# Two-layer transformer stack with a chunked recurrence: small triangular inverses taken off TensorE, in an eight-pair loop

## What is computed

```python
def step(state, inp):                      # 16 heads of width 64
    r_t, w_t, k_t, v_t, aa_t, bb_t = inp   # aa = -kk, bb = kk * a
    sa = jnp.einsum('bhvk,bhk->bhv', state, aa_t)
    state = state * w_t[:, :, None, :] + sa[..., None] * bb_t[:, :, None, :] + v_t[..., None] * k_t[:, :, None, :]
    return state, jnp.einsum('bhvk,bhk->bhv', state, r_t)
y = scan(step, ...); y = group_norm(y) * lnx_w + lnx_b; out = (y + bonus) * g
```

## Time and profile before

| | us |
|---|---|
| median of the three runs (lowest, highest) | 2082.74 (2081.55, 2086.68) |
| profiled execution, its own time | 2081.08 |
| its span | 2079.3 |
| PE busy | 2031.4 (98%) |
| PEld busy | 1678.5 (81%) |
| DVE busy | 1139.5 (55%) |
| ACT busy | 536.0 (26%) |
| POOL busy | 1178.7 (57%) |

### The profile page before, as it was taken

How to read it: one execution, slowest core, us unless ns; L and a number is a source line. 1 busy time by engine, 2 the same in 40 slices (tenths; PEclk the granted TensorE clock), 3 DMA queues, 4 the chain that set the end, 5 groups by cost and what they waited for, 6 DMA issues and landing times.

```text
span 2079.3 us, 39898 instructions
## 1 busy us (share of the span) xinstructions
PE 2031.4 (98%) x16195; PEld 1678.5 (81%) x16195; DVE 1139.5 (55%) x1533; ACT 536.0 (26%) x1139; POOL 1178.7 (57%) x1175
## 2 busy tenths in 40 slices
PE   8999999999999999999999999999999999999998
PEld 6888888877877787788877888888886888888886
DVE  6878624466667654202068677666773655555312
ACT  2100002233434212313143133333223023333101
POOL 6888865634534475545547044433374867677764
PEclk9999999999999999999999999999999999999999
DMA  3323331353353422311323022111223432332231
GB/s 136 102 92 102 101 101 46 92 176 121 127 163 112 148 82 64 98 62 61 124 56 93 15 65 66 46 48 46 65 65 124 133 101 81 101 99 90 89 112 56
DMA packets 181243, 190.28 MB, mean 92 GB/s; under 512 B 8526, under 2 KB 162269, under 8 KB 180829
## 3 DMA queue, kind: packets, MB, share of 16 engines
q1 hardware_dynamic: 172288, 181.81, 27.6%
q10 hardware_dynamic: 8796, 6.21, 1.0%
HBM read 179.56 MB, written 8.44 MB: 90 GB/s over the span
## 4 chain that ended last, share of the span: by engine, by line
PE 61%; DVE 3%; issue 1%; POOL 1%; DVEq 1%; POOLq 1%; ACT 0%; ACTq 0%
PE bank L915 8%; PE bank L916 8%; PE bank L917 8%; PE bank L1592 7%; PE bank L1553 3%; PE bank L1405 3%; PE bank L1421 2%; PE bank L1423 2%; PE bank L1422 2%; PE bank L1690 2%; PE bank L1327 1%; PE bank L1328 1%; PE bank L1329 1%; PE bank L1080 1%; PE bank L1294 1%
## 5 line engine op out<-in xcount | busy, mean ns | idle before, releaser
L740 POOL TENSOR_SCALAR whi<-raws 128x1024 fp32r<-128x1024 f32 (+5 forms) x312 | 321.0, 1029 | 284.9 <-PE bank L1082 166.8
L746 POOL TENSOR_TENSOR wlo<-raws,whi 128x512 fp32r<-128x512 f32 (+5 forms) x312 | 400.8, 1285 | 0.0
L745 POOL TENSOR_TENSOR wlo<-raws,whi 128x512 fp32r<-128x512 f32 (+5 forms) x312 | 373.4, 1197 | 46.0 <-issue 3.0
L915 PE MATMUL bank<-hbuf,whi 128*128 128x512 f32 (+2 forms) x840 | 329.4, 392 | 1.8 <-POOL wlo L746 1.8
L917 PE MATMUL bank<-hbuf,wlo 128*128 128x512 f32 (+2 forms) x840 | 327.8, 390 | 0.0
L916 PE MATMUL bank<-hbuf,whi 128*128 128x512 f32 (+2 forms) x776 | 303.0, 390 | 0.0
L649 POOL TENSOR_TENSOR spare<-ones 1x1 f32<-1x1 f32 x92 | 21.4, 233 | 298.5 <-PE bank L917 208.2
L915 PEld LDWEIGHTS bank<-hbuf,whi 128*128 128x128 f32 (+2 forms) x840 | 157.1, 187 | 37.0 <-POOL wlo L746 3.1
L917 PEld LDWEIGHTS bank<-hbuf,wlo 128*128 128x128 f32 (+2 forms) x840 | 157.1, 187 | 34.1
L916 PEld LDWEIGHTS bank<-hbuf,whi 128*128 128x128 f32 (+2 forms) x776 | 145.2, 187 | 31.1
L672 POOL TENSOR_SCALAR lg2L<-lg 128x128 fp32r<-128x128 f32 x8 | 2.4, 298 | 221.7 <-DMA lg<-in_g 221.7
(11 more groups left out here) (544 smaller groups left out, 4747.1 us busy)
## 6 DMA issues: line engine op xcount, KB each, us to landing
adaw<-in_w_ada SPq DMA_DIRECT2D x64, 384.0 KB, 4.3
raws<-in_w_up SPq DMA_DIRECT2D x22, 1024.0 KB, 4.9
raws<-in_w_in SPq DMA_DIRECT2D x41, 512.0 KB, 3.9
raws<-in_w_in SPq DMA_DIRECT2D x18, 1024.0 KB, 5.0
raws<-in_pool_w_in SPq DMA_DIRECT2D x16, 1024.0 KB, 5.4
raws<-in_mla_w_in SPq DMA_DIRECT2D x10, 1024.0 KB, 6.2
raws<-in_pool_w_out SPq DMA_DIRECT2D x8, 1024.0 KB, 5.1
raws<-in_mla_w_out SPq DMA_DIRECT2D x8, 1024.0 KB, 5.4
```

Source lines behind the costliest of these rows:

```text
L740: G.tensor_scalar(h_, r_, 1.0, 1.0, ALU.mult, ALU.mult)
L745: G.tensor_tensor(first[0], first[1], f32(first[2]), ALU.subtract)
L746: G.tensor_tensor(last[0], last[1], f32(last[2]), ALU.subtract).then_inc(raw_split, 1)
L915: M.matmul(dst, wh, acts[k][0], start=(first and k == 0), stop=False)
```

## The change

1. The 16x16 diagonal blocks are no longer inverted by products. `LEVELS` has four levels with five products instead of nine with 13. The gram "D" is masked and packed by DVE (`diagonal_blocks`) into 128x128, written to DRAM by a DMA on ACT's queue in runs of 16 elements, and read back so that each of 64 partitions holds one 16x16 block (`blocks_gathered`); DVE inverts the 64 blocks elementwise (`inverted_blocks`), the result and its transpose go to DRAM (`blocks_kept`) and come back in runs of 16 elements, 2048 of them (`blocks_spread`), and DVE spreads them over the 64x64 layout (`spread_blocks`).
2. "D" is computed inside gates(q), after 6 of its 48 matmuls (`D_AFTER`), instead of in slot 1 of the chain. DVE signals `rk.ab` as soon as the two operands of D are there.
3. The other steps of `prepare` are placed anew: slots 1, 2, 6, 7, 9, 10, 12, 14, 16, 17, 19, 21 hold one product each, the others none (before: 1 to 17, 19, 20, 21, 23).
4. Tiles of the decay and key part that lay in SBUF now lie in PSUM: sums of decays and `grown` in bank 5, key lengths, directions and modified keys in bank 3, the deviation in bank 4. The decay's constant factor goes into the scales of ACT's exponentials (one DVE instruction less, one sigmoid on ACT more); `kk` is no longer stored.
5. DVE's group norm is cut in two: `deviations(p)` (reciprocal, first product) after the decayed keys, `finished(p)` inside the next preparation.
6. Waits and banks follow (gate banks (0, 7) for all later pairs; `key_norms` waits for `rk.bon`, the chain for `gn.x`).

The core of the diff, with the other edits cut:

```diff
-    (("DA", "D", "N2"), ("D", "DA", "A2")),
-    (("N2", "A2", "A4"), ("A2", "U", "U")),
-    (("A4", "U", "V"),),
-    (("A4", "V", "V"),),
-    (("A4", "V", "V"),),
-    (("V", "I", "W"), ("E16", "V", "Z")),
+    (("E16", "V", "Z"),),
     (("W", "Z", "V"), ("Z", "W", "W")),
     (("E32", "V", "Z"),),
     (("W", "Z", "last"),),
...
-GATES_BESIDE = {3: (0, 20), 6: (20, 34), 15: (34, 48)}
+GATES_BESIDE = {2: (0, 20), 5: (20, 34), 8: (34, 48)}
+D_AFTER = 6
+BLOCKS_KEPT_AT = (3, 1)
...
             def gates(q):
-                for n in range(3 * DT):
+                for n in range(D_AFTER):
                     gate_part(q, n)
-                pe.wait_ge(sem("rk.bonus"), q)
-                pe.wait_ge(sem("rk.y"), q)
+                gram(q, "D")
+                for n in range(D_AFTER, 3 * DT):
+                    gate_part(q, n)
+                pe.wait_ge(sem("rk.sig"), q + 1)
...
+            def blocks_gathered(q):
+                act.wait_ge(sem("blk.d"), q + 1)
+                act.dma_start(blocks_in[q % 2].rearrange("(c p j) -> p c j", c=CHUNKS, p=P),
+                              diagonal.rearrange("p (c j) -> p c j", c=CHUNKS)).then_inc(sem("blk.kept"), 16)
+                act.wait_ge(sem("blk.kept"), 16 * (q + 1))
+                act.dma_start(blk, blocks_in[q % 2].rearrange("(n x) -> n x", n=64)).then_inc(sem("blk.in"), 16)
+            def blocks_kept(q):
+                act.wait_ge(sem("blk.x"), q + 1)
+                act.dma_start(blocks_out[q % 2].rearrange("(w n x) -> n w x", w=2, n=64),
+                              hf[0:64, 0:2 * BLK * BLK].rearrange("n (w x) -> n w x", w=2)).then_inc(sem("blk.out"), 16)
+            def blocks_spread(q):
+                act.wait_ge(sem("blk.out"), 16 * (q + 1))
+                act.dma_start(hf[:, S + P:S + 3 * P].rearrange("p (x j) -> p x j", j=BLK),
+                              blocks_out[q % 2].rearrange("(x p j) -> p x j", p=P, j=BLK)).then_inc(sem("blk.back"), 16)
             def take_gates(q):
                 take_gate(q, 0)
+                if q >= 2:
+                    blocks_gathered(q)
                 take_gate(q, 1)
...
                     A.copy(sa[:, :], bank[5][:, cs]).then_inc(sem("sq.se"), 1)
+                    if p + 1 < PAIRS and c == BLOCKS_KEPT_AT[min(p, 1)]:
+                        blocks_kept(p + 1)
+                    if p + 1 < PAIRS and c == BLOCKS_KEPT_AT[min(p, 1)] + 1:
+                        blocks_spread(p + 1)
...
-                dve.wait_ge(sem("rk.sig"), q + 1)
-                V.tensor_scalar(lwd[:, :], lwd[:, :], -float(np.exp(-0.5)), None, ALU.mult)
-                dve.drain()
-                V.tensor_tensor_scan(cc[:, :], restart[:, :], lwd[:, :], 0.0, ALU.mult, ALU.add)
+                dve.wait_ge(sem("rk.rate"), q + 1)
+                V.tensor_tensor_scan(sums[:, :], restart[:, :], rates[:, :], 0.0, ALU.mult, ALU.add)
...
-                V.reciprocal(tile(sq, 1), tile(sq, 1))
-                V.tensor_tensor(kk[:, :], kk[:, :], tile(sq, 1), ALU.mult)
+                V.reciprocal(lengths[:, :], lengths[:, :])
+                V.scalar_tensor_tensor(lengths[:, :], Kr[:, :], pcol[q % 3][:, 5:6], lengths[:, :], ALU.mult, ALU.mult)
```

More of the change, by code:

```diff
@@ L1751, in _ @@
             pe.wait_ge(sem("lora.act"), 2)
+            gram(0, "D")
             for step in range(1, 24):
@@ L2119, in sigmoids @@
                 act.wait_ge(sem("rk.pc"), q + 1)
-                A.activation(lwd[:, :], lora_bank(q)[:, :], ACT.Sigmoid, bias=pc[:, 3:4])
+                rate = A.activation(lwd[:, :], lora_bank(q)[:, :], ACT.Sigmoid, bias=pc[:, 3:4])
+                if q:
+                    rate = A.activation(bank[5][:, :], bank[5][:, :], ACT.Sigmoid, bias=pc[:, 3:4])
+                rate.then_inc(sem("rk.rate"), 1)
                 A.activation(aa[:, :], bank[7][:, :], ACT.Sigmoid, bias=pc[:, 4:5]).then_inc(sem("rk.sig"), 1)
@@ L2193, in deviations @@
             def deviations(p):
                 act.wait_ge(sem("gn.v"), p + 1)
[L2195 removed]
+                A.activation(deviation_tile(p)[:, :], bank[4][:, :], ACT.Sqrt, scale=1.0 / 64, bias=gneps_c[:, 0:1])\
                     .then_inc(sem("gn.s"), 1)
@@ L2898, in prepared, with diagonal_blocks @@
                     decayed_keys(1)
-                for k in range(5, len(LEVELS)):
+                    decayed_queries(1)
+                    dve.drain()
+                for k in range(len(LEVELS)):
                     take_level(k)
                 dve.drain()
+                if q == 0:
+                    diagonal_blocks(1)
+            def diagonal_blocks(q):
+                dve.wait_ge(sem("rk.block"), q + 1)
+                masked(inv_D, bank[1], "up16")
+                dve.drain()
+                V.tensor_reduce(diagonal.rearrange("p (c j) -> p c j", c=CHUNKS),
+                                inv_D[:, :].rearrange("p (c b j) -> p c j b", c=CHUNKS, j=BLK), AX.X, ALU.add)\
+                    .then_inc(sem("blk.d"), 1)
@@ new lines, in inverted_blocks, with square, times @@
+            def inverted_blocks(q):
+                dve.wait_ge(sem("blk.in"), 16 * (q + 1))
+                V.memset(blk[:, 0:BLK * BLK:BLK + 1], 1.0)
+                fours = hf[0:64, 0:4 * 68].rearrange("n (b r) -> n b r", r=68)
+                quad = [64, 4, 2]
+                t2 = blk_half[:, 0:8].rearrange("n (b j) -> n b j", j=2)
+                V.tensor_tensor(t2, fours[:, :, 1:2].to_broadcast(quad), fours[:, :, 18:20], ALU.mult)
+                dve.drain()
+                V.tensor_tensor(fours[:, :, 2:4], fours[:, :, 2:4], t2, ALU.add)
+                dve.drain()
+                V.tensor_tensor(t2, fours[:, :, 35:36].to_broadcast(quad), fours[:, :, 2:19:16], ALU.mult)
+                dve.drain()
+                V.tensor_tensor(fours[:, :, 3:20:16], fours[:, :, 3:20:16], t2, ALU.add)
+                dve.drain()
+                for m in (4, 8):
+                    n, cube = BLK // (2 * m), [64, m, m, m]
+                    def square(r0, c0):
+                        first = r0 * BLK + c0
+                        return hf[0:64, first:first + m * BLK].rearrange("n (i c) -> n i c", c=BLK)[:, :, 0:m]
+                    def times(lefts, rights):
+                        for b in range(n):
+                            terms = blk_terms[:, b * m ** 3:(b + 1) * m ** 3]
+                            V.tensor_tensor(terms.rearrange("n (i j k) -> n i j k", i=m, j=m),
+                                            lefts[b].unsqueeze(2).to_broadcast(cube),
+                                            rights[b].rearrange("n k j -> n j k").unsqueeze(1).to_broadcast(cube),
+                                            ALU.mult)
+                        dve.drain()
+                    corners = [(b * 2 * m, b * 2 * m) for b in range(n)]
+                    upper = [square(r, c + m) for r, c in corners]
+                    times([square(r, c) for r, c in corners], upper)
+                    half = blk_half[:, 0:n * m * m]
+                    V.tensor_reduce(half, blk_terms[:, 0:n * m ** 3].rearrange("n (x k) -> n x k", k=m), AX.X, ALU.add)
+                    dve.drain()
+                    times([half[:, b * m * m:(b + 1) * m * m].rearrange("n (i k) -> n i k", k=m) for b in range(n)],
+                          [square(r + m, c + m) for r, c in corners])
+                    for b in range(n):
+                        V.tensor_reduce(upper[b], blk_terms[:, b * m ** 3:(b + 1) * m ** 3]
+                                        .rearrange("n (i j k) -> n i j k", i=m, j=m), AX.X, ALU.add)
+                    dve.drain()
+                V.tensor_copy(blk_t.rearrange("n (j i) -> n j i", j=BLK), blk.rearrange("n (i j) -> n j i", j=BLK))\
+                    .then_inc(sem("blk.x"), 1)
```

260 lines of the change are left out of this document (147 added, 113 removed).

## The result

The changed kernel took 2100.57 us (median of five runs, 2097.44 to 2105.93), the kernel before 2082.74 in the same comparison (five runs, 2080.21 to 2086.85). The ratio is 1.008, 95% interval 1.0062 to 1.0098: slower by 0.8%, where 2070 was forecast, and outside the range (2052 to 2092). The profiled execution has a span of 2098.8 us against 2079.3, 19.5 us more.

A forecast was written before the change was run, and what follows sets the result against it. PE, busy 98% of the span, was taken as the bound. Six pairs at -3.2 us (-19) and the start at +6.5 gave -12.5 from 2081.08, 2068.6; runs' median 1.7 higher: 2070 us, range 2052 to 2092.

The forecast's parts named there:

- The gain of the products: Chain: fewer level products and D moved out, less the cost of empty slots, save 5.2 us a chain.
- Gates +1.5: Gates: D comes back at 0.93 us, shape changes cost about 0.1, and D waits 0.5 for its input.
- D late: Rival, gates: PSUM forms no faster beside POOL, D waits 2 us more, 2082; chance 0.15 shared with clock and more slip.
- The inverse is there 5.9 us into the chain: Loop chain: DVE's inversion takes 5.9 us, ready before ACT reaches its wait at 6.2.
- late block rival: Rival: transfers and inversion late in the chain, each us a us per pair; likely near 2088, 2104 at worst; chance 0.22.
- comes at 7.35, DVE is ready at 7.3: Loop chain: gram qb, waiting for bank 0's mask behind the inversion, comes at 7.35 us with DVE ready at 7.3.
- The clock rival: Rival: with eleven slots empty the clock falls once a chain, costing 1.7 us, 2081; chance 0.15 shared with D late.
- The start, +6.5: Ahead of the loop and in chain 0: unhidden round trips of pairs 0 and 1 and low clock cost 6.5 us together.
- Chain 6, counted as a sixth ordinary pair: Chain 6 was taken to gain like the other loop chains, -4.7 us, among six pairs of -3.2 us each.
- Whatever leaves PE shortens the loop: Whole loop: PE sets the pace, so work taken off it shortens the loop unless something it hid comes out.
- Chain 7, "stays": Last chain: it has no preparation, so its time was to change by 0.
- Short runs: Last transfer, 2048 runs of 64 bytes back: 3.0 us expected, between 1.8 and 7.2.

The follow-up runs named there:

- e3: The changed kernel with the four transfers and the elementwise inversion left out for all pairs: 2060.67 us, ratio 0.9888 to the kernel before.
- e7: Changed kernel, but pairs 0, 1, 7 inverted by old products; pairs 2 to 6 with transfers three and four on SP, A's masks inside the inversion, new slots: 2068.97 us.
- e9: As e7, but transfers three and four on ACT's queue in chunks 1 and 2: 2098.56 us, ratio 1.007 to the kernel before.
- e10: As e9, but the two waits one chunk later on ACT's queue, in chunks 2 and 3: 2072.6 us, ratio 0.9943 to the kernel before.
- e1: The changed kernel with transfers three and four issued by SP instead of ACT for pairs 1 to 7: 2105.56 us, ratio 1.01 to the kernel before.
- e8: The changed kernel with two products more, result unused, in empty slots 4 and 5 of chains 1 to 5: 2098.98 us, ratio 1.0056 to the kernel before.
- e5: As e1, with gram qb moved from slot 6 to 8 and the turns and qk behind it placed later: 2099.82 us, ratio 1.0057 to the kernel before.
- e4: The changed kernel with the four transfers and the inversion left out for pairs 0 and 1 only: 2076.26 us, ratio 0.9954 to the kernel before.
- e2: The changed kernel with pair 6's deviation kept in SBUF and chain 7 waiting only for ACT's square root: 2100.47 us, ratio 1.0076 to the kernel before.

## Why the prediction was wrong, point by point

**The gain of the products: right.** "-5.2 a chain" is 29.44 to 24.24 in e3, and 24.8 to 25.0 in e7 with the whole path in it for five pairs.

**Gates +1.5: right in size.** PE's row in the gates of pair 4:

```profile
1355.09 1.15 PE L1611 MATMUL bank<-aT,bT 64*64 64x64 f32 x32 [0.26 <-DVE bT L2847]
```

D waits 0.26 us for `bT` (0.5 forecast) and takes 0.93; wide part and gates grew by 1.63. The products of the key part, now with one input in PSUM, took 0.69 to 0.76 us with POOL busy beside them, so the rival "D late" did not come.

**"The inverse is there 5.9 us into the chain": the step that failed in the loop.** It is there at 7.6 in chain 2, 7.3 to 8.05 in all. Two terms were too small. The read was put at 2.4 us and took 3.8, so DVE starts 0.83 us into the chain. The inversion was put at 5.9 and took 6.8, mostly since a 64x512 product with a broadcast input took 1.01 to 1.03 us, not the 0.69 of a whole tile. With ACT's wait from 6.1 that is the late block rival in its place, ACT's queue: one of the signs named for it, ACT's state copy of chunk 1 waiting for DVE, is the row above. I had put the slack there at none (5.9 against 6.2), and e9 and e10 show that this one number decides. The forecast for `qb`, "comes at 7.35, DVE is ready at 7.3", was wrong in the same way (8.8, the masks' end), and e1 shows that mending ACT's queue alone only uncovers it. The price is a stop of 1.6 to 2.4 us in each of chains 1 to 5, against 0.5 allowed, and the half clock behind four of them. The rival had been given a chance of 0.22 and 2104 at worst. That sum does not follow: a pair that loses 5 us where it gained 3.2 is 8.2 us worse, and over six pairs, with 4 at the start, this is 53 us and not 34.

**The clock rival: right in price (1.7 a chain), wrong in cause for this kernel.** I had it follow from eleven empty slots. As this kernel has them, at most three in a row, they do nothing (e3). The stops do: four of five chains are 1.2 to 2.9 us longer than the one whose clock stayed up (27.14 to 28.74 against 25.89), and e8, which shortens the stops, takes it back. The rival was not empty, though: with five empty slots in a row the clock fell in two of five chains without any stop (e5).

**The start, +6.5: it was +15.1.** PE's five stops, then DVE's inversion for pair 0:

```profile
1146.05 1.97 PE L1611 MATMUL bank<-rT,bT 64*64 64x64 f32 x32 [8.33 <-DVE inv_E L2787]
...
1164.94 3.68 PE L1611 MATMUL bank<-hf 64*64 64x64 f32 x64 [6.82 <-DVE hf L2931]
...
1178.11 0.33 PE L1696 MATMUL bank<-rhs,xT 64*64 64x64 f32 x4 [2.24 <-ACT rhs L2292]
...
1187.39 1.97 PE L1611 MATMUL bank<-rT,bT 64*64 64x64 f32 x32 [4.47 <-DVE inv_E L2787]
...
1200.41 1.45 PE L1611 MATMUL bank<-inv_D,inv_E 64*64 64x64 f32 x32 [3.18 <-DVE inv_D L2975]
```

```profile
1135.75 0.55 DVE L2988 TENSOR_TENSOR hf<-hf 64x8 f32<-64x8 f32 x1
...
1137.74 1.51 DVE L3006 TENSOR_TENSOR inv_D<-hf 64x64 f32<-64x64 f32 x2
...
1144.34 0.37 DVE L3024 COPY hf<-hf 64x256 f32<-64x256 f32 x1
```

The first stop was to end at 1143 and ends at 1146.05. The inversion began about when forecast (1135.75 against 1135.4) but, with its first part beside POOL's work, it took 9.0 us where 6.5 was counted; its two 64x64 products took 1.51 us, 0.44 in chain 2. The second stop was put at 7 and is 6.82. Between the two, PE lost 2 us more, most of it because two products behind the first stop ran at half clock (1.97 and 1.95 us), and the forecast had a spell of low clock only behind the second. So the tail of the preparation begins at 1164.94 where 1160.2 was said. With 2.3 us of low clock behind the second stop (1.7 forecast) and 3.3 for D, its packing and its write (2.3 forecast), the first right side of chain 0 comes at +9.4 (1178.11 against 1168.71), where +3.0 was said: 6.4 of the 8.6 us that the forecast missed here.

In chain 0 the two stops that were put at 4.3 and 3 us are 4.47 and 3.18: right. The clock fell behind both of them; against e4's chain 0 (24.19) the 37.32 us are 9.9 of three stops and 3.2 of clock. Behind four of the five stops the first product ran slower (1.97, 3.68 for 64 blocks, 1.97 and 1.45, against 1.15 for 32 and 2.08 for 64). The steps that failed are the length of the inversion beside POOL and the clock, which fell behind four stops and not behind two.

**Chain 6, counted as a sixth ordinary pair: the step that failed at the end.** Of its -4.7 nothing was to be had, even without the serial path: in e3 this stage takes 38.15 us against 38.27 before, with PE standing for 6.73 us until POOL is through. "Whatever leaves PE shortens the loop" does not hold in this stage. The new path then costs 1.3 us here. POOL slows the inversion, as DVE's timeline shows, with PE's row behind it:

```profile
1555.20 1.69 DVE L3006 TENSOR_TENSOR inv_D<-hf 64x512 f32<-64x512 f32 x1
```

```profile
1562.32 0.48 PE L1696 MATMUL bank<-state,aT 64*64 64x64 f32 x4 [5.78 <-ACT state L2305]
```

The second product of this kind took 1.94 us and the inversion 11.4, and PE stood for 5.78 at the state and 2.08 for POOL at the end; most of this stands where e3's single wait for POOL stood. **Chain 7, "stays": +3.6**, since the divided group norm keeps bank 4 until DVE has multiplied by it (e2). I had not followed either into the last two pairs.

**Short runs.** The read back of 2048 runs of 64 bytes took 3.5 us (median of the seven above; 2.8 to 4.8 over all eight), 3.0 with SP issuing it in e7, near the estimate of 3.0 and under the bound of 7.2. The Trainium skill, "DMA: Bandwidth & Descriptors", Specifications, calls transfers under 512 bytes read-modify-writes. The page gives no time for such a transfer. Here the same 128 KB took 2.4 us out in runs of 1 KB and 3.5 back in runs of 64 bytes, and DVE waited for the way back only once, in chain 0. The transfer that made the loop chains late was not one of short runs: it was the read of 64 rows of 1 KB (3.8 to 4.3 us in four pairs).

## What to carry to other kernels

Work taken off the bounding engine and put in series through DMA and a second engine must arrive before every consumer on every queue asks for it. Write each consumer's asking time beside the arrival, and treat a slack under 1 us as a wait; here one chunk later on a queue was 26 us. Then look at the pairs at both ends of the loop apart: nothing hides the path at the start, and at the end another engine may set the pace, so that work taken off the bounding engine of the loop gives nothing there.

## What the hardware showed that I had not expected

- The same idle time of PE, and even the same rows, were followed by full clock in one chain and by half of it in another. Eleven gaps of 0.2 to 0.3 us with at most three empty slots in a row left the window clock at 1.00 in all of e3's chains 1 to 5. Five empty slots in a row, with no gap over 0.31 us, were followed by half clock in chains 3 and 5 of e5; behind the same five in its chains 1, 2 and 4 the clock stayed full. One stop of 1.6 to 3.3 us mostly brought half of the clock, but stops of 1.94 us (changed, chain 2) and 1.53 us (e1, chain 2) left it at 1.00, while a stop of 1.64 (changed, chain 5) and the same 1.53 us in e1's chain 3 were followed by products at half clock (1.95 us).
- DVE's 64x512 product of two SBUF inputs took 1.01 to 1.03 us with POOL idle and 1.69 to 1.94 beside POOL; its masks of PSUM tiles took 0.67 to 0.69 in the same stretch of chain 6. The Trainium skill, "SBUF — State Buffer", SBUF: two separate sides, says that VectorE and GpSimd share a port pair, that whichever starts first holds it for the whole instruction, and that a VectorE instruction with two SBUF inputs needs it against a GpSimd instruction that reads SBUF. These rows agree.
- SP's strip loads are not early by nature: a wait of 10 us put ahead of them in the one chain where they are due lengthened PE's wait for POOL at the stage's end from 2.08 us to 11.44 (e1) and 11.53 (e5).
